# Rotary part of a paged cache attention: one fp32 product against three products in the rounded type

## What is computed

```python
def mla_keys(ckv, kpe, w_kb, k_norm_g):
    kn = jnp.einsum('blr,rhe->blhe', ckv, w_kb)
    kp = jnp.broadcast_to(kpe[:, :, None, :], kn.shape[:-1] + (MLA_ROPE,)).astype(kn.dtype)
    return rmsnorm(jnp.concatenate([kn, kp], axis=-1), k_norm_g)
...
    def page_step(carry, phys):
        c = lat_pool[phys]
        kr = rope_pool[phys]
        return update(carry, scores(c, kr), c), None
```

## Time and profile before

| | us |
|---|---|
| median of 3 runs | 3636.77 (3636.39 to 3642.57) |
| the profiled execution | 3643.21 |
| its span on the core | 3641.4 |
| the cache attention's two stretches with pages in work | 550 to 1058 and 2355 to 2863 |

### The profile page before, as it was taken

The page is one execution under the profiler, slowest core; times in us unless marked ns, Lnnn a source line. Parts: engine busy times, 40 slices in busy tenths (PEclk is TensorE's granted clock), DMA queues, the critical chain, the costliest instruction groups (busy, mean ns, idle before and its releaser), DMA issues. The chain is left out here.

```text
span 3641.4 us, 67385 instructions
## 1 busy us (share of the span) xinstructions
PE 3072.2 (84%) x26442; PEld 2723.6 (75%) x26442; DVE 1933.0 (53%) x3127; ACT 1353.8 (37%) x2146; POOL 1124.6 (31%) x720
## 2 busy tenths in 40 slices
PE   7668879999988879888885788699999788798888
PEld 7568548888877459787884784498888684697878
DVE  5463454555546455489155544454545465454991
ACT  3412344444433233333344133344444331333333
POOL 0031000999910000055501300029998000001554
PEclk8889889999988779999987899799999886798999
DMA  5101203111114146443350021122112230564433
GB/s 162 36 3 31 78 13 87 39 50 30 52 37 126 47 133 173 110 131 107 109 162 13 3 69 40 29 71 55 34 41 64 72 106 8 156 162 109 131 105 113
DMA packets 444032, 282.35 MB, mean 78 GB/s; under 512 B 64686, under 2 KB 439256, under 8 KB 443082
## 3 DMA queue, kind: packets, MB, share of 16 engines
q1 hardware_dynamic: 441492, 276.85, 26.9%
q10 hardware_dynamic: 2232, 1.26, 0.2%
HBM read 258.75 MB, written 19.29 MB: 76 GB/s over the span
## 5 line engine op out<-in xcount | busy, mean ns | idle before, releaser
L290 POOL TENSOR_TENSOR w_rests<-w_ring,w_heads 128x2048 fp32r<-128x2048 f32 (+1 forms) x76 | 306.9, 4042 | 1291.6 <-ACT w_heads L284 1291.6
L1245 PE MATMUL key_banks<-w_kb_head,latent_T_head 128*128 128x352 f32 x1536 | 518.8, 338 | 0.0
L1245 PE MATMUL key_banks<-w_kb_rest,latent_T_head 128*128 128x352 f32 x1536 | 496.6, 323 | 0.0
L1245 PE MATMUL key_banks<-w_kb_head,latent_T_rest 128*128 128x352 f32 x1536 | 496.2, 323 | 0.0
L1065 POOL TENSOR_TENSOR rwkv_state_tmp<-rwkv_state,vec 128x1024 f32<-128x1024 f32 x64 | 153.7, 2402 | 681.4 <-DMA rwkv_state<-in_state_rwkv_dram 676.5
L284 ACT CAST w_heads<-w_ring 128x2048 fp32r<-128x2048 f32 (+1 forms) x180 | 325.4, 1811 | 66.7 <-DMA w_ring<-in_w_in_dram 24.1
L1388 DVE TENSOR_REDUCE w_kb<-key_sq 128x8 f32<-128x1024 f32 x256 | 309.5, 1209 | 0.0
L1374 DVE TENSOR_TENSOR latent_T_rest<-turn_bank,latent_T_head 128x256 fp32r<-128x256 f32 x256 | 108.7, 425 | 367.0 <-ACT w_kb L1306 366.9
L1305 ACT CAST latent_T_head<-turn_bank 128x256 fp32r<-128x256 f32 x256 | 95.5, 373 | 558.5 <-PE turn_bank L1225 558.5
L1245 PEld LDWEIGHTS key_banks<-w_kb_rest,latent_T_head 128*128 128x128 f32 x1536 | 291.1, 190 | 0.0
L1245 PEld LDWEIGHTS key_banks<-w_kb_head,latent_T_head 128*128 128x128 f32 x1536 | 290.5, 189 | 0.1
(11 more groups left out here) (559 smaller groups left out, 7689.9 us busy)
## 6 DMA issues: line engine op xcount, KB each, us to landing
w_ring<-in_w_in_dram SPq DMA_DIRECT2D x48, 1024.0 KB, 5.5
w_ring<-in_ffn_w_up_dram SPq DMA_DIRECT2D x88, 512.0 KB, 5.0
latents<-in_cache_kv_latent_dram SPq DMA_DIRECT2D x256, 128.0 KB, 2.0
w_ring<-in_w_gate_dram SPq DMA_DIRECT2D x48, 512.0 KB, 4.0
w_ring<-in_ffn_w_down_dram SPq DMA_DIRECT2D x32, 384.0 KB, 3.7
w_ring<-in_ffn_w_down_dram SPq DMA_DIRECT2D x32, 320.0 KB, 4.1
rope_keys<-in_cache_k_rope_dram SPq DMA_DIRECT2D x256, 32.0 KB, 1.8
ssm_native<-in_state_ssm_dram SPq DMA_DIRECT2D x16, 512.0 KB, 7.1
```

The source lines that it names most:

```text
L290: ops.tensor_tensor(rests[:, slot, 0:tiles * P], ring[:, slot, 0:tiles * P], heads[:, slot, 0:tiles * P].bitcast(F32), ALU.subtract).then_ ...
L1245: last = nc.tensor.matmul(kbank[:, 3 * x + n, 0:KB], c[:, x, r * P:(r + 1) * P], w[:, r, cols], start=r == 0 and m == 0, stop=r == 1 and m ...
```

## The change

The rotary keys get heads and rests like the latents. `ch` and `cl` widen from 256 to 384 columns: ACT's one instruction rounds 384 columns of `turn_bank` where two instructions read 256 and 128 (the latter of 64 partitions), and DVE's one subtraction takes 384 columns instead of 256. The 64 partitions of `turn_bank` that the rotary transpose does not write are set to 0 once. The rotary queries of all samples get heads (ACT) and rests (DVE) once per layer ahead of the loop, with a wait on PE for them. The one fp32 product with 64 rows and 32 columns becomes three F32R products with the same rows and columns.

```diff
@@ cache_attention
-        ch, cl = st.sb("latent_T_head", [P, 2, KVRANK], F32R), st.sb("latent_T_rest", [P, 2, KVRANK], F32R)
+        TW = KVRANK + P
+        ch, cl = st.sb("page_T_head", [P, 2, TW], F32R), st.sb("page_T_rest", [P, 2, TW], F32R)
+        qrh, qrl = st.sb("q_rope_head", [ROPE, NB * 32], F32R), st.sb("q_rope_rest", [ROPE, NB * 32], F32R)
...
-        kpT = reuse(1344, 2, P)[0:ROPE, :, :]
...
+        cleared, qr_headed, qr_split = st.sem("turn_bank_cleared"), st.sem("q_rope_head_ready"), st.sem("q_rope_split")
@@ tensor: body
-                        nc.tensor.matmul(kbank[:, bank, o:o + 32], kpT[:, x, :], k.qr[:, ds(b, 1), :].rearrange("p o c -> p (o c)"),
-                                         start=False, stop=True, skip_group_check=True).then_inc(scored, 1)
+                        at = b * 32
+                        kph, kpl = ch[0:ROPE, x, KVRANK:TW], cl[0:ROPE, x, KVRANK:TW]
+                        for m, (c, q) in enumerate(((kph, qrh), (kph, qrl), (kpl, qrh))):
+                            last = nc.tensor.matmul(kbank[:, bank, o:o + 32], c, q[:, ds(at, 32)], start=False, stop=m == 2, skip_group_check=True)
+                        last.then_inc(scored, 1)
@@ tensor: ahead of the loop
+                pe.wait_ge(cleared, 1)
                 turn(0, 0, 0, 0)
                 pe.wait_ge(w_split, 1)
+                pe.wait_ge(qr_split, 1)
@@ scalar
+                nc.scalar.copy(qrh[:, :], k.qr[:, :, :].rearrange("p b c -> p (b c)")).then_inc(qr_headed, 1)
...
-                    nc.scalar.copy(ch[:, x, :], xbank[:, 0:2 * P])
-                    nc.scalar.copy(kpT[:, x, :], xbank[0:ROPE, 2 * P:3 * P]).then_inc(headed, 1)
+                    nc.scalar.copy(ch[:, x, :], xbank[:, 0:TW]).then_inc(headed, 1)
@@ vector
+                nc.vector.memset(xbank[ROPE:P, KVRANK:TW], 0.0).then_inc(cleared, 1)
...
+                dve.wait_ge(qr_headed, 1)
+                nc.vector.tensor_tensor(qrl[:, :], k.qr[:, :, :].rearrange("p b c -> p (b c)"), qrh[:, :].bitcast(F32), ALU.subtract).then_inc(qr_split, 1)
...
-                    nc.vector.tensor_tensor(cl[:, x, :], xbank[:, 0:2 * P], ch[:, x, :].bitcast(F32), ALU.subtract).then_inc(t_kept, 1)
+                    nc.vector.tensor_tensor(cl[:, x, :], xbank[:, 0:TW], ch[:, x, :].bitcast(F32), ALU.subtract).then_inc(t_kept, 1)
```

## The result

The changed kernel takes 3677.8 us (median of 4 runs, 3672.9 to 3680.18) against 3636.58 of the kernel before, a ratio of 1.0107 with the interval 1.0093 to 1.0121: 34 to 44 us slower. The forecast was 3665.1 with a range of 3652 to 3681. The direction held and the time lies in the range. That it came so near is partly luck: one term of the sum was about 10 us too large, and another, of about 16 us, was missing.

The account below looks back on a forecast made before the run. PE was taken to bound 228 pages, ACT and DVE 28. PE's +29.6 us and ACT's -1.3, with DVE and setup at 0, sum to +28.3, on the median 3636.8 giving 3665.1 us; range 3652 to 3681.

Parts of the forecast that it names:

- What bounds: Attention: PE bounds 114 of 128 pages a layer; 14 end on a chain through ACT and DVE.
- 228 PE pages: Pages of both layers that end on PE alone, by which PE's added time per page was multiplied.
- The gap of 0.25 and the change of rows: Before the rotary product: 0.25 us instead of 0.16, caused by going from 128 to 64 rows; would stay.
- The third rival: Around the rotary products: F32R with 64 rows makes no change of rows, so gaps go; 3600.4 us, 8%.
- Its side term: Two transposes at a PE page's end: 0.17 us apart, would be 0.11 without change of rows; gain 0.06 more.
- PE's term: Rotary products on PE: three F32R instead of one fp32 add 0.13 us a page, +29.6 us.
- I take the step of the nearest row: Steps between the three rotary products: 0.13 us each, taken from L1249's own; 2 x 0.13 - 0.13 = 0.13 a page.
- the forecast's lower bound of 0.10: Page growth if the rotary products stream 0.013 us and step 0.115: 0.10 us a page, +22.8 us.
- the first rival: Rotary products: 64-row F32R loads run ahead among themselves, inner steps 0.112, page grows by 0.094; 3656.9 us, 14%.
- ACT and DVE: In 28 chain-bound pages ACT's one copy gains 0.045 us each, -1.3 us; DVE's wider subtraction costs 0.
- Elsewhere. No instruction of another stage changes: Stages outside the changed parts: no instruction changes, so no term was added to the sum.
- the second rival: Rotary products: short F32R products stream at a quarter of the rate, 0.053 us each; 3676.5 us, 16%.

Follow-up runs that it names:

- 3 products ahead of the changed kernel's loop: Changed kernel with 3 tiny products (12 PE instructions) added ahead of the first turn; 1.0121 of the kernel before (1.01 to 1.0141).
- 9 products on 128 rows: Changed kernel with its three rotary products over 128 rows and 9 tiny products ahead of the first turn; 0.9903 of the kernel before.

## Why the prediction came out as it did

- **What bounds.** Mostly held. PE bounds the plain and the value pages, and ACT and DVE bound pages 5 and 6. The count of 228 PE pages was 14 too high, though: page 14 of seven samples a layer grew by 0.01 only. In the kernel before, the load for L1274 waits there for DVE's L1420, 0.9 us in six pages of the first layer; in the changed kernel that wait is gone, filled by the longer page. The setup cost nothing that can be seen: PE waits 12.2 us for the first page where it waited 12.3.
- **The gap of 0.25 and the change of rows.** This held and is shown: with 64 rows the gap stayed in F32R, with 128 it went, in both types. The third rival fell. Its side term, the 0.17 between the transposes as an effect of the rows, was a wrong reading.
- **PE's term, forecast +29.6 us, measured about +19.5** (13.7 + 5.0 + 0.1, and 0.75 for the eight pages at the returns). The step that was mis-sized is "I take the step of the nearest row": both inner steps were given 0.13. In the trace the loads of the products are 0.11 apart, and only the first step, behind the first load of 64 rows, is 0.13; the way back is 0.19. The reading behind it, that a load of 64 rows doesn't run beside the matmul before it, holds for the first load alone. A page grew by 0.094, which is below the forecast's lower bound of 0.10 and is the figure of the first rival, though that rival put both steps at 0.112. The 14 pages that did not grow take another 1.3.
- **ACT and DVE.** The copy of 384 columns reads 0.48 us (0.49 forecast), DVE's rest 0.56 (0.57), and a chain page is mostly 0.04 shorter (0.045 forecast): -1.7 us in all, where -1.3 was forecast.
- **"Elsewhere. No instruction of another stage changes"** was where the sum was incomplete. No term looked at what the change does to the place of the code. It added 11 to 16 us at four returns of the loop: 8.8 by the stops in front of long products, the rest by the clock's 1.2 GHz behind them. This, not the 0.053 of streaming that the second rival asked for, is why the time came out near that rival's 3676.5: the steps in the trace rule that rival out.
- **The trace did hold the sign.** The kernel before waits at each return. In the view of the earlier trace rows this line stands in the place of the "...":

```profile
PE turn_bank L1224 <- issue: 1.8, 2, 1.0
```

## What to carry to other kernels

Count an fp32 product of few columns by its loads: two, where heads and rests take three products and three loads. At 32 columns the rounded type lost by one load; from how many columns on it pays was not tried here. A product with 64 rows amid ones of 128 costs more by the change of rows than by anything it computes, and zeros in the other 64 rows were worth 1.7% of the whole kernel. Before a difference of some microseconds is put down to an edit in a loop with much PE code, look behind the loop's return for waits on "issue", and shift the code once with harmless instructions to see what is left.

## What was not expected of the hardware

- The loads of 64 rows follow each other by 0.11 us like those of 128 rows; only the first behind products of 128 rows does not run ahead, which makes the first step 0.13 and those behind it 0.11.
- PE's code comes in packets of 16 KB. By where the loop starts, a return costs nothing (3.69 us for the page), 1 to 1.7 us, or that and a further stop of 1.1 to 2.9 us; with 3 products ahead of the changed kernel's loop it was one stop of 4.1 to 4.6 us. Behind the stops of over 2 us TensorE ran 3.4 or 6.8 us at the 1.2 GHz level.
- A loop whose code is kept needs no fetch at all at its return: 36 packets fewer over the program. How much code is kept was not measured; the kernel with 9 products on 128 rows lost nothing at the first return of each layer (its queue has no packet of code from 720 to 858 us) and over 1.6 us at the second, behind which code was fetched anew. Why the second turn kept what the third did not stays open.
